# Output projection in 512-column form with its second half tile by tile between the norms, the MLP begun on three token tiles, and three reorderings at earlier boundaries

## The chip, the core and the metric

One core of a Trainium2 chip runs the whole program. The metric is the device time of one execution in microseconds (us).

## The reference, cut to what matters

One layer over 512 prompt tokens and 8 x 16 sample tokens, 640 in all, that is five tiles of 128, with 1024 channels:

```python
xn = rms_norm(x, norm_mix_pre);  z = xn @ w_in            # split into the inputs of three branches
y_fox = forgetting attention (8 heads);  y_lru = gated linear recurrence;  y_gla = gated linear attention
mix = sum_r sigmoid(gate_r(xn)) * (y_r @ w_branch[r])
mix = mix @ w_out                                          # the output projection
x = x + rms_norm(mix, norm_mix_post)
hn = rms_norm(x, norm_mlp_pre)
x = x + rms_norm(square(relu(hn @ w_up)) @ w_down, norm_mlp_post)
```

Keys, values, log forgets, convolution tails and recurrent states are outputs as well.

## The kernel before

Each engine runs its own list in order and waits on semaphores. Every fp32 product is made of three matmuls of a high and a low part (activations `XH`, `XL` or `YH`, `YL`; weights `WH`, `WL`). A weight block of 0.5 MB goes through one of two slots `s`: SP loads it into `raw[s]`, ACT casts it to `WH[s]` (`hi`, L1060), DVE subtracts for `WL[s]` (`lo`, L1465). SP loads block b+2 when `lo` of b is done; `hi` of b+2 waits until PE has finished block b. Blocks are numbered in program order.

`block` (L564) is the common form: a 128-column block of weights stays in the array and 320 tokens move, 24 matmuls for each half `h` of the tokens into `Z[0]` and `Z[1]` (PSUM banks 0 and 1). `down` (L955) is the other form: 128 tokens stay, 512 columns of weights move, one block holds two channel tiles (`kp`) of 512 columns, and the five tiles of tokens have a bank each, `DBK` (banks 2 to 6).

**Start.** Five tiles are normed and turned into `XH`, `XL` (`norm_turn` L580, `norm_hi` L1072, `norm_lo` L1471). Block 0 gives the forget inputs. PE then turns the cached log forgets (`cp_raw`, L595), and DVE copies them (L1518) and sums them up (L1521, a scan). Blocks 1 to 3 are q, k and v of head 0. After block 1 PE turns the log forgets `lfT`, after block 2 their sums `cT`. SP's list: loads 1 and 2, a wait for the sums (`ff_c`) and their store to `nc_new`, `nc_past`, load 3, head 0's cached keys (four DMAs, L364), the two stores of the log forgets (L417, L418), load 4, a wait for these stores, head 0's cached values and the sums back as rows (L359, L371 to L374), load 5. In block 4 head 0's attention begins: DVE does `lo` of block 5, key transposes (L1548), then the soft maximum; PE's `turn_p` (L669) waits for it (L1591).

**Merges.** After each branch `merge_begin(r)` runs two blocks of gates, and `merge(r)` alternates blocks `y_r @ w_branch` with gate blocks; its first branch block waits for the whole `y_r`. Before `merge(1)` PE turns `last` (L775), the recurrence's final columns, and ACT copies them to `LS` (L1275) for four stores.

**Output projection.** `MIX` is split into `YH`, `YL` (L1387, L1859). Eight blocks of `block` give the product transposed, ACT copies each into `OTB`, and PE turns every token tile back (`natural`, L918) into two banks. For each tile then: `root` on ACT (square with sum L1081, root L1082), scaling on DVE (L1874), the add to `X2` on POOL (L1024; the last tile's on DVE, L1885), a second `root`, scaling for the MLP (`normed`, L1483), `norm_turn`, `norm_hi`, `norm_lo`.

**MLP.** Four groups of eight `up` blocks (L940, 320 tokens moving) and eight `down` blocks. `up` waits for three tiles before its first half and for all five before its second.

Of the kernel before, what the change touches and what calls it, by code (L numbers as in the profile page):

```python
# [25 lines left out]
P = 128  # L26
# [70 lines left out]
def build(nc, ins, outs):  # L97
# [50 lines left out]
    with ExitStack() as ctx:  # L148
# [70 lines left out]
        def sems(names):  # L219
# [39 lines left out]
        mix_hi, mix_split, nat_pe, nat_free, x_again, nat_root, x2_ready, x2_last, x2_root = sems(  # L259
            "mix_hi mix_split nat_pe nat_free x_again nat_root x2_ready x2_last x2_root")  # L260
# [20 lines left out]
        (WG, LG, GQ, TG, Y2, RA, RX, AA, TH, A2, MM, UU, HH, XC, XP, LS) = carve(  # L281
            A0, (2, P), (T,), (T,), (T,), (T,), (T,), (T,), (T,), (T,), (T,), (T,), (T,), (T,), (T,), (XPW + 1,), (D,))
# [9 lines left out]
        OTB, X2, G1, G2, G3 = carve(A0, (KT, T), (NT, D), (D,), (D,), (D,))  # L292
        HS1, NJ, TM = carve(0, (2, D), (D,), (2, D))
# [5 lines left out]
        DBK = bank[2:7]  # L299

# [26 lines left out]
        ORD = (0, 1, 4, 2, 3)  # L327


        @blk.sync  # L330
        def _(sp):
# [77 lines left out]
            sp.wait_ge(ff_c, 1)  # L409
            sp.dma_start(nc_new, ncT[0:FOX_HEADS, :]).then_inc(scr_out, 16)  # L410
            sp.wait_ge(cp_scan, 1)
            sp.dma_start(nc_past, cpast[0:FOX_HEADS, :].rearrange("h (b s) -> h b s", s=PAST)).then_inc(scr_out, 16)
            load(Lin(B_FOX + 2), (B_FOX + 2) % 2, w_fox(Lin(0), 2))
            for q in range(P // TB):
                load_cache_k(slice(0, 1), 0, q)
            sp.wait_ge(lfn_sb, 1)
            sp.dma_start(flf_p[0, 0].rearrange("(t p) h -> p t h", p=P), lfn[:, 0:NTP, :]).then_inc(stored, 16)  # L417
            sp.dma_start(flf_s[0].rearrange("b t h -> (b t) h"), lfn[:, NTP, :]).then_inc(stored, 16)  # L418
            load(Lin(B_FOX + 3), (B_FOX + 3) % 2, w_fox(Lin(1), 0))
# [133 lines left out]
        def _(pe):  # L553
# [1423 lines left out]
```

## Time and profile before

| what | value |
|---|---|
| median of three runs | 1577.84 us (1577.53 to 1578.05) |
| the profiled execution, its own time | 1578.37 us |
| span of its trace | 1576.6 us |
| PE busy | 1508.9 us, 96% |
| DVE, ACT, POOL busy | 692.0, 622.2, 34.3 us |
| DMA | 143.41 MB, 91 GB/s over the span |

The span runs from the first to the last instruction in the trace; the own time has 1.8 us more around it. PE is busy in nearly all of the span, so what can be moved is where it is not, and where its clock is at the lower of two levels (a granted clock of 0.50 is 1.2 GHz, 1.00 is 2.4 GHz).

### The profile page before, as it was taken

Reading aid. Unit: us, or ns where it says so; the run is one execution under the profiler, and the core shown is the slowest. Engines: PE = TensorE matmul, PEld = TensorE weight load, DVE = VectorE, ACT = ScalarE, POOL = GpSimd, SP = SyncE. Lnnn points to the kernel's source line nnn. Section 1 sums busy time; section 2 is a strip of 40 time slices with the busy share of each in tenths; the row PEclk is TensorE's granted clock in tenths of the full one; section 3 lists DMA queues with packets and bytes.
Section 4 is the critical chain, followed back from the end, with each engine's and each line's share of the span. In section 5 each row is a group of like instructions: output and inputs, shape, how many; then the busy total and the mean of one; then the engine's idle time right before and its main releaser. Section 6 shows DMA issues by size and latency. Waiting matters only on the chain.

```text
span 1576.6 us, 26085 instructions
## 1 busy us (share of the span) xinstructions
PE 1508.9 (96%) x9854; PEld 1411.0 (89%) x9854; DVE 692.0 (44%) x1189; ACT 622.2 (39%) x1123; POOL 34.3 (2%) x39
## 2 busy tenths in 40 slices
PE   6799999999999989999999999997799999999996
PEld 6799999889999979998998899997798998998985
DVE  7355555532368762334445442333532322323234
ACT  6133333321277751244464432134451341431523
POOL 1000000000000000000000000001100000000003
PEclk9899999999999989999999999998799999999998
DMA  3976778222222212232332232521122222222222
GB/s 115 163 147 147 154 154 154 76 78 80 71 60 68 82 54 80 71 104 73 96 110 88 75 92 73 186 68 40 39 68 80 80 79 68 80 80 69 78 80 80
DMA packets 281350, 143.41 MB, mean 91 GB/s; under 512 B 73654, under 2 KB 268919, under 8 KB 281292
## 3 DMA queue, kind: packets, MB, share of 16 engines
q1 hardware_dynamic: 281300, 142.72, 34.5%
q8 instruction: 34, 0.56, 0.2%
q14 instruction: 16, 0.13, 0.0%
HBM read 129.86 MB, written 12.84 MB: 91 GB/s over the span
## 4 chain that ended last, share of the span: by engine, by line
PE 82%; DVE 8%; ACT 4%; issue 3%; DMA 1%; SPq 1%; DVEq 0%; ACTq 0%; POOL 0%
PE psum L564 45%; PE psum L940 14%; PE psum L955 14%; PE psum L658 1%; PE psum L688 1%; DMA w_raw<-in_w_in_dram 1%; DVE arena L1483 1%; DVE arena L1725 1%; ACT arena L1232 1%; DVE arena L1780 1%; PE psum L669 1%; PE psum L877 1%; PE psum L875 1%; PE psum L630 1%; ACT w_hi L1060 1%
## 5 line engine op out<-in xcount | busy, mean ns | idle before, releaser
L564 PE MATMUL psum<-XH,w_hi 128*128 128x320 f32 x1424 | 453.8, 319 | 6.5 <-DVE w_lo L1465 3.6
L564 PE MATMUL psum<-XH,w_lo 128*128 128x320 f32 x1424 | 443.6, 311 | 0.0
L564 PE MATMUL psum<-XL,w_hi 128*128 128x320 f32 x1424 | 443.4, 311 | 0.0
L1465 DVE TENSOR_TENSOR w_lo<-w_raw,w_hi 128x1024 fp32r<-128x1024 f32 x185 | 226.4, 1224 | 417.8 <-ACT w_hi L1060 417.0
L1060 ACT CAST w_hi<-w_raw 128x1024 fp32r<-128x1024 f32 x185 | 193.6, 1047 | 338.2 <-PE psum L955 166.3
L564 PEld LDWEIGHTS psum<-XH,w_hi 128*128 128x128 f32 x1424 | 270.9, 190 | 18.9 <-issue 9.8
L564 PEld LDWEIGHTS psum<-XL,w_hi 128*128 128x128 f32 x1424 | 270.9, 190 | 0.6
L564 PEld LDWEIGHTS psum<-XH,w_lo 128*128 128x128 f32 x1424 | 270.5, 190 | 0.0
L564 PE MATMUL psum<-YH,w_hi 128*128 128x320 f32 x512 | 160.4, 313 | 3.1 <-DVE YL L1859 2.0
L940 PE MATMUL psum<-XH,w_hi 128*128 128x320 f32 x512 | 159.1, 311 | 1.5 <-DVE fix L1929 1.5
L564 PE MATMUL psum<-YL,w_hi 128*128 128x320 f32 x512 | 159.6, 312 | 0.0
L564 PE MATMUL psum<-YH,w_lo 128*128 128x320 f32 x512 | 159.6, 312 | 0.0
L940 PE MATMUL psum<-XL,w_hi 128*128 128x320 f32 x512 | 158.9, 310 | 0.0
L940 PE MATMUL psum<-XH,w_lo 128*128 128x320 f32 x512 | 158.8, 310 | 0.0
L955 PE MATMUL psum<-w_lo,YH 128*128 128x512 f32 x320 | 124.5, 389 | 0.0
L955 PE MATMUL psum<-w_hi,YH 128*128 128x512 f32 x320 | 124.5, 389 | 0.0
L955 PE MATMUL psum<-w_hi,YL 128*128 128x512 f32 x320 | 124.5, 389 | 0.0
L1065 ACT ACTIVATE arena<-psum 128x320 f32<-128x320 f32 (+1 forms) x112 | 48.5, 434 | 145.1 <-PE psum L564 145.0
L564 PEld LDWEIGHTS psum<-YH,w_hi 128*128 128x128 f32 x512 | 97.6, 191 | 4.0 <-issue 3.5
L940 PEld LDWEIGHTS psum<-XH,w_hi 128*128 128x128 f32 x512 | 96.8, 189 | 2.0 <-DVE fix L1929 1.9
L564 PEld LDWEIGHTS psum<-YL,w_hi 128*128 128x128 f32 x512 | 97.5, 190 | 0.0
L1906 DVE TENSOR_TENSOR YL<-arena,YH 128x320 f32 x64 | 31.5, 492 | 150.3 <-ACT YH L1422 150.3
(254 smaller groups left out, 1748.7 us busy)
## 6 DMA issues: line engine op xcount, KB each, us to landing
w_raw<-in_w_in_dram SPq DMA_DIRECT2D x88, 512.0 KB, 3.7
w_raw<-in_w_up_dram SPq DMA_DIRECT2D x32, 512.0 KB, 4.0
w_raw<-in_w_down_dram SPq DMA_DIRECT2D x32, 512.0 KB, 3.5
w_raw<-in_w_branch_dram SPq DMA_DIRECT2D x24, 512.0 KB, 3.8
arena<-in_cache_fox_k_dram SPq DMA_DIRECT2D x32, 256.0 KB
arena<-in_cache_fox_v_dram SPq DMA_DIRECT2D x8, 1024.0 KB
out_dram<-arena SPq DMA_DIRECT2D x26, 256.0 KB, 2.5
arena<-in_state_gla_dram SPq DMA_DIRECT2D x4, 1024.0 KB, 5.4
```

The lines of the kernel that those rows point to most:

```text
L564: mm = pe.matmul(Z[h][:, 0:HT], w[s][:, k, :], x[:, k, h * HT:(h + 1) * HT], start=(k == 0 and i == 0), stop=(k == KT - 1 and i == 2))
L630: mm = pe.transpose(TBK[j % 2][:, (i - 4 * j) * P:(i - 4 * j + 1) * P], src[:, par, tok(i % NT)], idf[:, :])
L658: pe.matmul(S[:, 0:w], QT[:, par, tok(t)], KTt[:, par, 0:w], start=True, stop=False)
L669: mm = pe.transpose(TBK[2][:, i * P:(i + 1) * P], SP[:, p % 2, i * P:(i + 1) * P], idf[:, :])
L688: mm = pe.matmul(O[:, 0:P], KVN[:, i, :], pt[:, i * P:(i + 1) * P], start=(i == 0), stop=(i == t))
L875: pe.matmul(O[:, 0:GLA_DV], AT[:, t, :], VN[:, t, :], start=True, stop=False)
L940: mm = pe.matmul(Z[h][:, 0:HT], w[s][:, k, :], x[:, k, h * HT:(h + 1) * HT], start=(k == 0 and i == 0), stop=(k == KT - 1 and i == 2))
L955: mm = pe.matmul(DBK[t], y[:, 2 * kp + k, tok(t)], w[s][:, k, :], start=(kp == 0 and k == 0 and i == 0), stop=(kp == KP - 1 and k == 1 and ...
L1060: act.copy(WH[s][:, :, :], raw[s][:, :, :]).then_inc(w_hi, 1)
L1065: act.activation(dst, Z[h][:, 0:HT], ACT.Copy, scale=scale).then_inc(z_free[h], 1)
L1465: dve.tensor_tensor(WL[s][:, :, :], raw[s][:, :, :], WH[s][:, :, :].bitcast(F32), ALU.subtract).then_inc(w_lo, 1)
L1906: dve.tensor_tensor(YL[:, bass.ds(i * 2 + s, 1), half], UQ[:, half].unsqueeze(1), YH[:, bass.ds(i * 2 + s, 1), half].bitcast(F32), ALU.sub ...
```

## The change

The output projection takes the form of `down`. `out_first` makes the first 512 output columns of all five tiles in `DBK`; `out_second(t)` makes the other 512 for one tile at a time in `Z[(t + 1) % 2]`. The second half's four weight blocks all stay resident: two in the slots, two in the columns of `XH`, `XL` that belong to tiles 3 and 4 (`spare`), which are not needed until those tiles are normed. The tiles come out in natural order, so `OTB` and `natural` go. Squares of the first halves are summed ahead (`out_sq`, `out_bias`); each tile's norms run on ACT and DVE while PE makes the next tiles, with `norm_turn(t - 2)` inside `out_second(t)`. POOL's adds go to DVE. The first two `up` blocks start on their first token half between the norms of tiles 3 and 4.

The three reorderings: at the start the cached log forgets are turned before block 0, `lfT` and `cT` are turned inside block 2, and SP issues load 3, head 0's keys and load 4 ahead of the stores of the sums; `merge` begins with `late_block`, which makes all but the last channel tiles of both halves before it waits for the rest of `y_r`; the turning and storing of `last` moves behind `merge(1)`, its buffer `LS` into the gates' tile, and the next branch no longer waits for those stores.

```diff
 # PE, start
+            for j in CP_ORD:                       # (2, 3, 0, 1)
+                pe.wait_ge(nt_free, 2 * NT if j < 2 else 2 * NT - 2)
+                ... four transposes of cp_raw into bank[2 + j], cp_pe
             block(Lin(0), 0, XH, XL)
-            ... sixteen transposes of cp_raw
             block(Lin(1), 1, XH, XL)
-            ... transposes of lfT
-            block(Lin(2), 0, XH, XL)
-            ... transposes of cT
+            block(Lin(2), 0, XH, XL, (turn_lf, None))   # turn_lf: waits ff_lf, turns lfT; waits ff_c, turns cT
             block(Lin(3), 1, XH, XL)
 # SP, start
-            sp.wait_ge(ff_c, 1); sp.dma_start(nc_new, ...); sp.wait_ge(cp_scan, 1); sp.dma_start(nc_past, ...)
             load(Lin(B_FOX + 2), ...)
             for q in range(P // TB): load_cache_k(slice(0, 1), 0, q)
+            load(Lin(B_FOX + 3), ...)
+            sp.wait_ge(cp_scan, 1); sp.dma_start(nc_past, ...); sp.wait_ge(ff_c, 1); sp.dma_start(nc_new, ...)
             sp.wait_ge(lfn_sb, 1)
             sp.dma_start(flf_p ...); sp.dma_start(flf_s ...)
-            load(Lin(B_FOX + 3), ...)
 # DVE, start: cp8 is negated before the scan of c8; lo(Lin(3)) comes before the copy of lfn
 # PE, merges
+            def late_block(b, s, y_sem, early, y_early, y_count):
+                pe.wait_ge(w_lo, (b + 1).v)
+                for ks in (range(early), range(early, KT)):
+                    pe.wait_ge(y_sem, y_count if ks.stop == KT else y_early)
+                    for h in range(2):
+                        if ks.start == 0: pe.wait_ge(z_free[h], b.v)
+                        for k in ks: ... three matmuls into Z[h]
+                        if ks.stop == KT: mm.then_inc(z_done[h], 1)
-            merge(0, y_done, 5 * FOX_HEADS)
+            merge(0, y_done, FOX_HEADS - 1, 5 * (FOX_HEADS - 1), 5 * FOX_HEADS)
+            merge(1, yl_done, LRU_N - 1, LRU_N - 1, LRU_N)      # now ahead of the transposes of last
-            merge(1, yl_done, LRU_N)
-            merge(2, gy_done, 2 * GLA_H)
+            merge(2, gy_done, 2 * (GLA_H - 1), 2 * (GLA_H - 1), 2 * GLA_H)
 # ACT, merge(1): its two tanh of gate block 1 move ahead of the wait for h_ready; the copy to LS follows merge(1)
 # PE, output projection
+            def out_first(kp):
+                b = B_OUT + kp
+                pe.wait_ge(w_lo, b + 1); pe.wait_ge(mix_split, 2 * kp + 2)
+                for t in range(NT):
+                    for k in range(2): ... three matmuls, 512 columns, into DBK[t]
+                    if kp == KP - 1 and t < NT - 1: mm.then_inc(out_a, 1)
+                mm.then_inc(z_done[1], 1)
+            def out_second(t):
+                if t >= 2: pe.wait_ge(out_free, t - 1)
+                order = (2, 3, 0, 1) if t == NT - 1 else (0, 1, 2, 3)
+                for at_, kp in enumerate(order):
+                    if t >= 2 and at_ == (2 if t == NT - 1 else 3): norm_turn(1, t - 2, HS1)
+                    for k in range(2):           # kp < 2: the weights are the slices spare(XH), spare(XL), 2 x 256 columns
+                        ... three matmuls, 512 columns, into OUTB[t]
+                    if t == NT - 1 and kp >= 2: mm.then_inc(z_done[1], 3 if kp == 2 else 1)
+                mm.then_inc(out_b, 1)
+            pe.wait_ge(out_free, NT - 1); pe.wait_ge(nt_free, 2 * NT + 2 * 3); pe.wait_ge(w_lo, B_MLP + 1)
+            up_half(B_MLP, B_MLP % 2, 0, UBK[0][0])
+            norm_turn(1, 3, HS1)
+            pe.wait_ge(w_lo, B_MLP + 2)
+            up_half(B_MLP + 1, (B_MLP + 1) % 2, 0, UBK[1][0])
+            norm_turn(1, 4, HS1)
+            pe.wait_ge(nt_free, 4 * NT)
+            for s in range(2): up_half(B_MLP + s, (B_MLP + s) % 2, 1, UBK[s][1])
 # ACT, output projection
+            for d in range(1, KP): hi(Lin(B_OUT + d), ...)
+            for kp in range(KP): ... hi of the second half's blocks; kp < 2 into spare(XH), the others after out_first(kp)
+            root_table()
+            for t in range(NT): ... square of DBK[t] with sum into SS
+            for t in range(NT + 1):
+                if t < NT: ... out_b: square of OUTB[t] with sum, root with bias HBIAS -> out_root
+                if t in (NT - 2, NT - 1): hi(Lin(B_MLP + t - (NT - 2)), ...)
+                if t >= 1: norm_hi(1, t - 1)
+                if t < NT: act.wait_ge(x2_ready, t + 1); root(X2[:, t, :], NJ[:, :], t, x2_root)
 # DVE, output projection
+            for t in range(NT + 1):
+                if t >= 1: dve.wait_ge(x2_root, t); normed(1, t - 1, X2[:, t - 1, :], G2[:, :], HS1)
+                if t < NT:
+                    dve.wait_ge(out_root, t + 1); rinv(t)
+                    ... two scalings of 512 columns into TM -> out_free; add of TM to X2 -> x2_ready
+                if t in (NT - 2, NT - 1): lo(Lin(B_MLP + t - (NT - 2)), ...)
+                if t >= 1: norm_lo(1, t - 1)
```

## Rows read from the trace of the kernel before

**Rows 1.** The page: PE's busy tenths in 40 slices of 39.4 us; groups of instructions (busy, mean ns).

```profile
PE   6799999999999989999999999997799999999996
...
L1465 DVE TENSOR_TENSOR w_lo<-w_raw,w_hi 128x1024 fp32r<-128x1024 f32 x185 | 226.4, 1224 | 417.8 <-ACT w_hi L1060 417.0
```

**Rows 2.** Busy time by stretch; the last three columns are granted clock, DMA share, GB/s.

```profile
55.10:58.40 3.30, 3.30 (x15) 3.30 (x14) 0.00 (x0) 0.00 (x0) 0.00 (x0) 0.50 1.47 121
316.00:323.30 7.30, 4.38 (x56) 3.61 (x56) 4.55 (x11) 2.48 (x7) 0.00 (x0) 1.00 0.38 110
...
1086.00:1119.80 33.80, 15.40 (x80) 13.05 (x80) 25.89 (x39) 22.24 (x44) 10.65 (x5) 0.65 0.00 0
1119.90:1123.20 3.30, 3.30 (x12) 3.30 (x13) 1.23 (x1) 0.09 (x1) 2.97 (x1) 0.50 0.10 29
1128.00:1175.00 47.00, 47.00 (x323) 47.00 (x322) 14.97 (x20) 25.17 (x47) 0.00 (x0) 1.00 0.22 67
1180.00:1230.00 50.00, 50.00 (x222) 41.44 (x221) 14.73 (x17) 8.14 (x8) 0.00 (x0) 1.00 0.23 75
```

**Rows 3.** PE in order of time: start, us, what; in brackets the idle time before it.

```profile
54.18 0.42 PE L564 MATMUL psum<-XH,w_hi 128*128 128x320 f32 x1 [1.42 <-DVE w_lo L1465]
...
78.54 0.33 PE L669 MATMUL psum<-ident,arena 128*128 128x128 f32 x1 [3.67 <-DVE arena L1591]
...
323.33 0.41 PE L564 MATMUL psum<-YH,w_hi 128*128 128x320 f32 x1 [1.06 <-DVE YL L1596]
...
578.27 1.87 PE L775 MATMUL psum<-ident,last 128*36 128x128 f32 x8 [6.39 <-DVE fix L1745]
```

**Rows 4.** SP's DMA issues in order of time, 45 to 65 us.

```profile
47.75 7.13 SPq L364 DMA_DIRECT2D arena<-in_cache_fox_k_dram  x4
54.92 3.16 SPq L417 DMA_DIRECT2D out_dram<-arena  x1
...
60.39 0.38 SPq L359 DMA_DIRECT2D arena<-in_cache_fox_v_dram  x1
...
64.84 3.08 SPq L336 DMA_DIRECT2D w_raw<-in_w_in_dram  x1
```

**Rows 5.** ACT in order of time, 30 to 92 us.

```profile
38.37 0.74 ACT L1115 ACTIVATE arena<-arena 8x640 f32<-8x640 f32 x1
...
72.66 1.05 ACT L1060 CAST w_hi<-w_raw 128x1024 fp32r<-128x1024 f32 x1 [8.39 <-DMA w_raw<-in_w_in_dram]
```

**Rows 6.** DVE in order of time, 30 to 92 us.

```profile
36.66 4.41 DVE L1521 TENSOR_TENSOR_SCAN arena<-arena 8x2048 f32<-8x2048 f32 x1
...
46.86 0.18 DVE L1534 COPY arena<-psum 128x40 f32<-128x40 f32 x1
```

**Rows 7.** ACT at the boundary between the recurrence and merge(1).

```profile
571.89 0.74 ACT L1255 ACTIVATE arena<-arena 128x640 f32<-128x640 f32 x1
...
577.19 1.28 ACT L1128 ACT_TABLE_LOAD   x1
578.48 0.77 ACT L1128 ACTIVATE gates<-psum 128x320 f32<-128x320 f32 x2
```

**Rows 8.** Groups of instructions, 1086 to 1120 us: busy, mean ns, idle before.

```profile
L1483 DVE SCALAR_TENSOR_TENSOR arena<-arena,small 128x1024 f32<-128x1024 f32 x5 | 11.0, 2204 | 0.2
L580 PE MATMUL psum<-ident,arena 128*128 128x128 f32 x40 | 9.0, 397 | 13.8 <-DVE XL L1471 9.1 <-DVE arena L1483 4.7
...
L1471 DVE TENSOR_TENSOR XL<-psum,XH 128x512 fp32r<-128x512 f32 x10 | 6.6, 682 | 1.4 <-ACT XH L1072 1.4
L1874 DVE SCALAR_TENSOR_TENSOR arena<-psum,small,arena 128x1024 f32<-128x1024 f32 x5 | 6.4, 1283 | 0.2
...
L1072 ACT CAST XH<-psum 128x512 fp32r<-128x512 f32 x10 | 5.8, 586 | 4.8 <-PE psum L580 4.8
L1081 ACT ACTIVATE arena<-arena 128x1024 f32<-128x1024 f32 x5 | 5.2, 1048 | 4.1 <-POOL arena L1024 2.7 <-DVE arena L1885 1.3
...
L1885 DVE TENSOR_TENSOR arena<-arena 128x1024 f32<-128x1024 f32 x1 | 1.2, 1225 | 0.0
```

More of the change, by code:

```diff
@@ L299, in build, with spare, by_256, norm_bank @@
         DBK = bank[2:7]
+        OUTB = [Z[(t + 1) % 2] for t in range(NT)]
+        UBK = ((Z[0], Z[1]), (DBK[0], DBK[1]))
+        def spare(v, kp, k, n=2):
+            return v[:, 4 * kp + 2 * k:4 * kp + 2 * k + n, T - 256:T]
+        def by_256(v):
+            return v[:, :, :].rearrange("p k n -> p (k n)").rearrange("p (a b) -> p a b", b=256)
+        def norm_bank(n, t, q):
+            if n == 0:
+                return bank[2 + 2 * (t % 2) + q]
+            return DBK[t] if q == 0 else bank[7]
         blk = ctx.enter_context(nc.Block())
@@ new lines, in _, with up_half @@
+            for kp in range(KP):
+                out_first(kp)
+            for t in range(NT):
+                out_second(t)
+            def up_half(b, s, h, bk):
+                for k in range(KT):
+                    for i, (w, x) in enumerate(((WH, XH), (WH, XL), (WL, XH))):
+                        mm = pe.matmul(bk[:, 0:HT], w[s][:, k, :], x[:, k, h * HT:(h + 1) * HT],
+                                       start=(k == 0 and i == 0), stop=(k == KT - 1 and i == 2))
+                mm.then_inc(z_done[h], 1)
@@ L1255, in lru_window @@
                     act.activation(MM[:, :], MM[:, :], ACT.Sqrt).then_inc(m_act, 1)
+                if not cur:
+                    for h in range(2):
+                        gate(1, Lin(1), b + 1, 1, h)
                 if cur:
@@ L1271, in _ @@
             lru_window(Lin(LRU_N), False, True)
[L1272 to L1273 removed]
+            merge(1)
             act.wait_ge(last_pe, 1)
+            act.wait_ge(mix_sum, 2 * KT)
             act.copy(LS[0:36, :], psum[0:36, 2:4, :].rearrange("p a b -> p (a b)")).then_inc(last_sb, 1)
[L1276 removed]
             def o_copy(h):
@@ new lines, in group @@
+            def group(g, last=False, done=0):
+                b = g * (2 * KT) + B_MLP
+                with step.loop(KT // 2 - done, 4) as i:
+                    for s in range(2):
+                        bb = (b + 2 * done).loop(2, i) + s
+                        hi(bb + 1, (b.c + s + 1) % 2)
+                        for h in range(2):
+                            up_half(Z[h], bb, bass.ds(i * 2 + (s + 2 * done), 1), (g * KT + 2 * done).loop(2, i) + s, h)
+                with step.loop(KT // 2 - last, 0) as i:
+                    for s in range(2):
+                        hi((b + KT).loop(2, i) + (s + 1), (b.c + KT + s + 1) % 2)
```

357 lines of the change are left out of this document (196 added, 161 removed).

## Prediction, made before the changed kernel was run

> **What bounds the kernel now.** I read the page first: PE is busy in nine tenths or more of nearly every slice, and the slices that fall short are the first three and two near 1100 us, with dips at the branch boundaries [rows 1]. So the kernel is bound by PE, and only PE's empty stretches, and those at the lower clock, can be won. The stretches by windows give their size. From 1086.0 to 1119.8 us PE is busy for 15.4 of 33.8 us, and with turning tiles only: this is the norms between output projection and MLP, where DVE has 25.9 and ACT 22.2 us of work [rows 2]. Then PE in order of time, read for the brackets: idle 3.67 us before 78.54, 1.06 before 323.33, 6.39 before 578.27 [rows 3]. Last SP's issues, because what PE waits for at 78.54 hangs on a load.
>
> Two prices serve throughout. In full stretches at a granted clock of 1.00, leaving out the one record cut off at each end, a 320-column matmul takes 47/321 = 0.146 us and a 512-column one 50/220 = 0.227 us [rows 2]. And idling can cost clock: behind an idle time of 1.42 us [rows 3] the clock stood at 0.50 for 3.3 us, and again behind the norms; in a stretch whose three gaps make 2.92 us, 1.06 of them the last, it stayed at 1.00 [rows 2, 3]. A stretch at the lower clock costs half its length, 1.6 us. Between none and one for each gap of 1 to 2 us, I count two for three.
>
> **Start.** Before, load 5 lands at 72.64 (its cast starts at 72.66), and 5.9 us later, at 78.54, PE gets head 0's first softmax tile: cast, `lo`, two key transposes, two soft maxima, one scaling, all queued on ACT and DVE behind that load [rows 3, 5]. What sets load 5 is SP: four key DMAs (7.13 us of issue), a store that takes 3.16 us to issue, load 4, a wait for the stores until the values go out at 60.39, load 5 at 64.84 [rows 4]. After the change the keys and loads 3 and 4 are issued from 24 to 38 us, beside PE's first blocks. SP is next needed when the copy of the log forgets (46.86 + 0.18 = 47.04) is done [rows 6]. That copy moves little. Before, DVE's scan ended at 41.07, `lo` 1.23 behind it, so the chain from there to the copy was 47.04 - 42.3 = 4.7 us [rows 1, 6]. After, the scan is done early and the chain starts with ACT's logarithm, which ended at 39.11 [rows 5]; block 0 starts some 1.4 us later (most of the sixteen transposes now stand before it, the same number less behind it), and `lo` 3 now stands in the chain: 39.1 + 1.4 + 4.7 + 1.2 = 46.4. From there SP needs 60.39 - 54.92 = 5.5 us to the values, so 51.9 [rows 4]. Load 5's landing is bounded: if the transfers take as long as from 60.39 to 72.64, 64.2; if only SP's issue (4.45 us later, 56.4) and the quickest load of some 4 us count, 60.5. I take the middle, 62.3: DMA was full there, and load 4's 0.5 MB, which overlapped the beginning of that stretch, is gone from it. PE gets its tile at 68.2, 10.3 us earlier; load 6 can come up to 0.8 us late for block 6, and I take off 0.7. **9.6 us won**, 7.6 to 12.1 by the bounds. The idle times before blocks 2 to 4 go too but are no extra: PE waits at the softmax tile instead, from about 64.
>
> **Merges 0 and 2.** `late_block` fills the 1.06 us before 323.33 with 42 matmuls that don't need the last head [rows 3]. At merge 2 PE does not wait, so nothing is won. Splitting off the last channel tile puts both halves' ends only 3 x 0.146 us apart, so the next block's first half waits for DVE's gating of the bank (about 0.5 us against 0.44): 0.1 to 0.2 us twice. **0.6 us won**, 0.3 to 1.1.
>
> **Merge 1.** PE was free at 578.27 - 6.39 = 571.9 [rows 3]. `late_block` needs both banks free, that is ACT's tanh of gate block 1, which now follows the square root (ends 572.63), with a table load of 1.28 and 0.4 us: 574.4 [rows 7]. Its 42 early matmuls last 6.2 us, beyond 578.1, when the last channel is split. So PE idles 2.5 us rather than 6.4 and then turning, and a stretch at 0.50 follows in both cases. The first branch block begins at 574.4 rather than 579.8 (after eight transposes): 5.4 us, and the eight transposes return after the merge for about 1.0 at full clock [rows 8]. The copy to `LS`, 1 us on ACT, delays the cast of the second block behind it, which has most of a 7 us block as cover; without that cover it would cost 1 us. The four stores on SP stand behind loads that run two blocks ahead. **4.4 us won**, 2.5 to 6.0.
>
> **Output projection and norms.** Before: 384 matmuls x 0.1464 = 56.2, the empty stretch 33.8, the stretch at 0.50 behind it 1.6: 91.6 us [rows 2].
>
> After: `out_first` is 120 x 0.227 = 27.2 us, begun about 0.7 us later because it waits for two split tiles, not one. Call its end S. ACT then has one cast 1.05, the root's table 1.5, five squares of 0.85: S + 6.9. So tile 0's second square starts at S + 7.1, though its matmuls end at S + 5.5. Per tile: ACT square with root 1.0; DVE scaling 1.28 in two parts and 0.2 for the reciprocal, add 1.23; ACT second root 1.5; DVE `normed` 1.28 and 0.2; PE eight transposes 1.0 (9.0/5 us at a clock of 0.65); ACT casts 0.59 each; DVE `XL` 0.68 each [rows 8]. (The mean of 2.2 us for `normed` has POOL's adds beside it. These go to DVE, so I take 1.28, its shape's time at L1874, and keep 2.2 as the bound.)
>
> The ring that repeats is add, second root, `normed`, scaling, add: 1.5 + 1.5 + 1.5 + 1.23 + hand-overs = 5.9 us. PE's share of a tile is 24 x 0.227 + 1.0 = 6.45. So from tile 2 on PE sets the pace: `out_second(4)` ends at S + 10.9 + 3 x 6.45 = S + 30.2. Then three gaps. Tile 3's add ends at S + 29.1, `lo` of the first `up` block and tile 2's two `XL` follow it on DVE: PE starts at S + 31.7, gap 1.5. `up` half 3.5, transposes 1.0: 36.2. Tile 4's add ends at 35.9, `lo` of the second block behind it: 37.2, gap 1.0. `up` half, transposes of tile 4: 41.7; its casts and `XL`: 43.4, gap 1.7. There the second halves begin and 48 matmuls of the MLP (7.0 us) are done. The rest of the MLP sees the same queues; the second-half weights' casts and loads have 6.8 us a block against a load of 4 and 2.3 for the two casts.
>
> Sum after: 0.7 + 27.2 + 43.4 - 7.0 + two stretches at 0.50 3.2 = 67.5. **24.1 us won.** Bounds: no stretch at 0.50 27.3; `normed` at 2.2 (the same recurrence gives S + 46.7) and three of them 19.2. The second half's weights in `spare` move as two runs of 256; no row shows that form. Nearest below is 0.227, above it two 320-column matmuls, 0.293, which on 60 matmuls would cost 4 us; a run of 256 is still contiguous, so I take nothing.
>
> Here a rule speaks for a larger gain. The rows show 0.227 us for each 512-column matmul with its own weight load [rows 2]. The Trainium skill, page "TensorE: Matmul & The Clock Gate", section "Back-to-back issue gap", gives about 131 ns as the sustained spacing at 512 columns in a real kernel. By that, 240 matmuls take 31.4 us rather than 54.5, and the sum would end 23 us lower (an estimate from that page). The 512-column matmuls of `down` in this trace don't bear it out, so it gets no chance of its own.
>
> **Sum.** 9.6 + 0.6 + 4.4 + 24.1 = 38.7 us. Against the profiled execution's own 1578.37 (span 1576.6 and 1.8 around it) that is 1539.7; the median of the runs lies 0.53 lower, so **1539 us**. All lows together give 29.6 (1548), all highs 46.5 (1531).
>
> **Rivals.** (a) The norms set the pace. DVE carries more than before, and the ring has only 0.5 us to spare against PE. If its memory-to-memory work stays at 2.2 us a tile, and the add is as slow as that too, each tile loses about 2 us more than PE hides: 8 us, 1547. For it: L1483's mean; against: POOL, beside which it was slow, falls idle. Chance 0.15. (b) The start is bound by DMA. Between 55 and 58 us the DMA share is over 1.4 [rows 2]; if load 5 lands 12.3 us after a later 55, not 62.3, only about 5 us are won there: 1544. Against it: the keys are gone from that stretch. Chance 0.12. (c) The short gaps cost no clock, in the tail and at merge 1: 3.2 + 1.6 less, 1534. For it, the stretch at 316. Chance 0.12. (d) Slower: the clock stays at 1.2 GHz through the projection. Each 512-column matmul would take some 0.2 us longer; about 190 of the 240 eat up the 39 us, and all of them give 1588 without the tail's fill. Against it: `down` holds 1.00 in the same form [rows 2]. Chance 0.02. (e) A wait I have not seen ties the projection to the old order, and only the other parts remain small: no change, 0.02.
>
> **How the numbers follow.** The forecast has 0.57, with a range of its own from 1534 to 1544. With (a), (b) and (c) the range 1529 to 1548 leaves out under 2 in 10. A measurement of this kernel can tell about 0.2%, 3 us: faster 0.96, same 0.02, slower 0.02.
>
> **What would show it.** Right: the span's two weak slices near 1100 disappear, three PE gaps of 1 to 2 us stand before the first full `up`, load 5's cast starts near 62, PE's idle time before merge 1 is near 2.5 us. Wrong: idle times inside `out_second` on `normed` (a), load 5's cast beyond 65 (b), clock below 1.00 in `out_first` (d). The weakest numbers are the landing of load 5 and how many gaps cost clock.

## The result and the profile after

| | before | after |
|---|---|---|
| median of four runs | 1577.68 us | 1534.03 us (1532.94 to 1537.67) |
| ratio, 95% interval | 1 | 0.9727 (0.971 to 0.9744) |
| profiled execution: own time, span | 1578.37, 1576.6 us | 1532.94, 1531.2 us |
| mean granted clock in it | 0.980 | 0.994 |

The change made the kernel faster, by 43.7 us in the medians and 45.4 us between the two spans. The profiled execution of after is the quickest of its four, and that of before (1578.37) lies above its four timed runs (1577.4 to 1578.05), so what is read from the two traces comes out 1.7 us larger than the medians. The executions of after whose clock is listed at 0.994, 0.994 and 0.991 had spans of 1531.2, 1532.2 and 1536.0 us; by an estimate, clock alone would make 0.003 x 1531 = 4.6 of the 4.8 us between the first and the last.

First the page of after, PE's slices and the grant, to set against [rows 1]; then PE of after in order of time, with the idle time in brackets, to set against [rows 3].

```profile
PE   6899999999999999999999999999999999999996
...
PEclk9999999999999999999999999999999999999999
```

```profile
67.74 0.47 PE L691 MATMUL psum<-ident,arena 128*128 128x128 f32 x1 [4.18 <-DVE arena L1687]
...
306.66 0.55 PE L691 MATMUL psum<-ident,arena 128*128 128x128 f32 x3 [1.60 <-DVE arena L1687]
...
554.06 0.39 PE L583 MATMUL psum<-XH,w_hi 128*128 128x320 f32 x1 [0.54 <-ACT gates L1200]
563.97 0.38 PE L769 MATMUL psum<-YH,w_hi 128*128 128x320 f32 x1 [2.63 <-ACT gates L1200]
...
900.03 1.28 PE L826 MATMUL psum<-ident,arena 128*128 128x128 f32 x10 [0.17 <-DVE arena L1876]
...
1013.18 0.47 PE L954 MATMUL psum<-w_hi,YH 128*128 128x512 f32 x1 [2.74 <-DVE YL L1955]
...
1071.65 0.38 PE L997 MATMUL psum<-XH,w_hi 128*128 128x320 f32 x1 [1.02 <-DVE XL L1566]
...
1076.91 0.42 PE L997 MATMUL psum<-XH,w_hi 128*128 128x320 f32 x1 [0.63 <-DVE w_lo L1560]
...
1083.13 0.42 PE L997 MATMUL psum<-XH,w_hi 128*128 128x320 f32 x1 [1.56 <-DVE XL L1566]
```

The two weak slices near 1100 us are gone; in their place stand three gaps that make 3.21 us. The same rows of before, and one pair ahead of merge 2, give the milestones. The row at 316.41 in before and 306.66 in after is the last head's softmax tile; it is called the later window below.

```profile
316.41 0.55 PE L669 MATMUL psum<-ident,arena 128*128 128x128 f32 x3 [1.60 <-DVE arena L1591]
...
564.61 0.38 PE L564 MATMUL psum<-XH,w_hi 128*128 128x320 f32 x1 [0.54 <-ACT gates L1128]
...
914.94 1.28 PE L786 MATMUL psum<-ident,arena 128*128 128x128 f32 x10 [0.17 <-DVE arena L1780]
...
1027.34 0.39 PE L564 MATMUL psum<-YH,w_hi 128*128 128x320 f32 x1 [2.00 <-DVE YL L1859]
...
1119.86 0.64 PE L940 MATMUL psum<-XH,w_hi 128*128 128x320 f32 x1 [1.47 <-DVE fix L1929]
```

| term | forecast | measured | from the rows |
|---|---|---|---|
| start | 9.6 | 9.75 | 316.41 - 306.66 |
| merges 0 and 2 | 0.6 | 0.80 | (564.61 - 554.06) less the start, all of it at merge 0: 914.94 - 900.03 = 14.91 ahead of merge 2, 14.90 behind it |
| merge 1 | 4.4 | 4.35 | (1027.34 - 2.00) - (1013.18 - 2.74) = 14.90, less the two above |
| output projection and norms | 24.1 | 30.5 | 45.4 less 14.90 |

The rest of the MLP is the same in both: from the last rows shown to the end it takes 1576.6 - 1119.86 = 456.7 us before, of which 1.6 are a stretch at the lower clock, and 1531.2 - 1083.13 = 448.1 after, which has 7.0 us of the MLP behind it by then. So the 30.5 belong to the stage.

Last, the queues and stretches of after that answer [rows 4, 5, 6, 8] and [rows 2]: SP's issues, ACT's cast of load 5, DVE's copy of the log forgets; groups of DVE in the tail; windows, whose last three columns are granted clock, DMA share and GB/s.

```profile
24.57 7.29 SPq L382 DMA_DIRECT2D arena<-in_cache_fox_k_dram  x4
...
45.65 0.39 SPq L436 DMA_DIRECT2D out_dram<-arena  x1
...
49.12 0.38 SPq L377 DMA_DIRECT2D arena<-in_cache_fox_v_dram  x1
...
52.67 4.21 SPq L354 DMA_DIRECT2D w_raw<-in_w_in_dram  x1
...
61.86 1.05 ACT L1132 CAST w_hi<-w_raw 128x1024 fp32r<-128x1024 f32 x1 [5.73 <-DMA w_raw<-in_w_in_dram]
...
45.44 0.18 DVE L1631 COPY arena<-psum 128x40 f32<-128x40 f32 x1
```

```profile
L1566 DVE TENSOR_TENSOR XL<-psum,XH 128x512 fp32r<-128x512 f32 x10 | 6.4, 685 | 2.0 <-ACT XH L1144 1.9
L1578 DVE SCALAR_TENSOR_TENSOR arena<-arena,small 128x1024 f32<-128x1024 f32 x5 | 6.4, 1285 | 0.2
L1988 DVE TENSOR_TENSOR arena<-arena 128x1024 f32<-128x1024 f32 x5 | 6.1, 1226 | 0.2
```

```profile
68.00:72.00 4.00, 4.00 (x17) 4.00 (x17) 1.50 (x5) 1.80 (x3) 0.00 (x0) 0.50 1.19 177
...
564.00:568.00 4.00, 4.00 (x18) 4.00 (x19) 3.21 (x7) 1.82 (x3) 0.30 (x1) 0.62 0.00 0
...
1013.20:1040.40 27.20, 27.20 (x120) 22.51 (x121) 11.43 (x12) 8.56 (x10) 0.00 (x0) 1.00 0.32 110
1040.40:1070.40 30.00, 30.00 (x146) 24.89 (x144) 20.50 (x39) 19.14 (x43) 0.00 (x0) 1.00 0.08 24
...
1072.00:1080.00 8.00, 7.37 (x53) 7.12 (x52) 7.43 (x10) 3.04 (x6) 0.00 (x0) 1.00 0.40 112
1080.00:1088.00 8.00, 6.44 (x46) 6.19 (x45) 2.27 (x4) 4.71 (x10) 4.37 (x1) 1.00 0.05 15
```

PE is busy through both halves of the projection without an idle row, and `normed` takes 1.285 us now that POOL does not add beside it, against 2.204 in [rows 8]. The grant is 1.00 through the tail in spite of its three gaps, and 0.50 to 0.62 behind the gaps at the softmax and at merge 1.

### The profile page after: what moved, and what is told of

Its sections match the earlier page's. It is cut to its first block, busy times and chain, and to the rows that moved or that the text cites. A ratio compares the mean times of both kernels' runs of the same rounds, so it can differ in the third digit from the quotient of the medians.

```text
span 1531.2 us, 25519 instructions
## 1 busy us (share of the span) xinstructions
PE 1487.6 (97%) x9670; PEld 1381.6 (90%) x9670; DVE 693.1 (45%) x1199; ACT 616.0 (40%) x1117; POOL 24.9 (2%) x35
## 4 chain that ended last, share of the span: by engine, by line
PE 84%; DVE 6%; ACT 4%; issue 3%; DMA 1%; SPq 0%; DVEq 0%; ACTq 0%
PE psum L583 41%; PE psum L997 15%; PE psum L1031 14%; PE psum L954 2%; PE psum L769 1%; PE psum L980 1%; PE psum L680 1%; PE psum L710 1%; DMA w_raw<-in_w_in_dram 1%; ACT arena L1304 1%; PE psum L691 1%; DVE arena L1876 1%; DVE arena L1821 1%; PE psum L917 1%; PE psum L915 1%
## 5 line engine op out<-in xcount | busy, mean ns | idle before, releaser
L1132 ACT CAST w_hi<-w_raw 128x1024 fp32r<-128x1024 f32 x181 | 189.6, 1048 | 317.7 <-PE psum L1031 166.4
L583 PEld LDWEIGHTS psum<-XL,w_hi 128*128 128x128 f32 x1424 | 268.5, 189 | 0.6
L583 PEld LDWEIGHTS psum<-XH,w_lo 128*128 128x128 f32 x1424 | 268.1, 188 | 0.0
L583 PE MATMUL psum<-YH,w_hi 128*128 128x320 f32 x336 | 103.8, 309 | 0.0
L583 PE MATMUL psum<-YL,w_hi 128*128 128x320 f32 x336 | 103.8, 309 | 0.0
L583 PE MATMUL psum<-YH,w_lo 128*128 128x320 f32 x336 | 103.8, 309 | 0.0
L997 PEld LDWEIGHTS psum<-XL,w_hi 128*128 128x128 f32 x512 | 96.1, 188 | 0.1
L997 PEld LDWEIGHTS psum<-XH,w_lo 128*128 128x128 f32 x512 | 96.1, 188 | 0.0
L1998 DVE TENSOR_TENSOR YL<-arena,YH 128x320 f32 (+1 forms) x64 | 31.5, 492 | 140.9 <-ACT YH L1504 140.8
L1137 ACT ACTIVATE arena<-psum 128x320 f32<-128x320 f32 x96 | 41.6, 434 | 114.8 <-PE psum L583 114.7
```

The lines of the kernel that those rows point to most:

```text
L583: mm = pe.matmul(Z[h][:, 0:HT], w[s][:, k, :], x[:, k, h * HT:(h + 1) * HT], start=(k == 0 and i == 0), stop=(k == KT - 1 and i == 2))
L997: mm = pe.matmul(bk[:, 0:HT], w[s][:, k, :], x[:, k, h * HT:(h + 1) * HT], start=(k == 0 and i == 0), stop=(k == KT - 1 and i == 2))
L1132: act.copy(WH[s][:, :, :], raw[s][:, :, :]).then_inc(w_hi, 1)
L1137: act.activation(dst, Z[h][:, 0:HT], ACT.Copy, scale=scale).then_inc(z_free[h], 1)
L1998: dve.tensor_tensor(YL[:, j, half], UQ[:, half].unsqueeze(1), YH[:, j, half].bitcast(F32), ALU.subtract).then_inc(u_done[h], 1)
```

## Experiments

Each kernel is the changed kernel with one edit. "Against after" is the ratio less 0.9727, times 1577.7 us; an interval of a ratio is about 2 us wide to each side, and after's own 2.7, so small differences are read from the milestones of the traces, one execution each.

| kernel | median, us | ratio to before, 95% interval | against after, us |
|---|---|---|---|
| start_undone | 1543.88 | 0.9785 (0.977 to 0.98) | +9.2 |
| start_queue_undone | 1542.13 | 0.9768 (0.9755 to 0.9782) | +6.5 |
| start_engines_undone | 1536.13 | 0.9733 (0.972 to 0.9746) | +0.9 |
| full_wait | 1537.85 | 0.9746 (0.9733 to 0.9759) | +3.0 |
| no_cover | 1569.54 | 0.9948 (0.9933 to 0.9963) | +34.9 |
| up_after_five | 1542.11 | 0.9769 (0.9756 to 0.9782) | +6.6 |
| adds_on_pool | 1538.87 | 0.9748 (0.9735 to 0.9762) | +3.3 |
| lo_on_pool | 1534.54 | 0.9727 (0.9714 to 0.9741) | 0.0 |
| softmax_first | 1530.45 | 0.9701 (0.9687 to 0.9714) | -4.1 |
| gate_early | 1530.69 | 0.97 (0.9687 to 0.9713) | -4.3 |
| combined | 1527.08 | 0.968 (0.9667 to 0.9693) | -7.4 |
| combined_two | 1527.09 | 0.9679 (0.9666 to 0.9692) | -7.6 |

**The start, undone whole (start_undone).** SP, PE and DVE issue the start in the order of before: the two edits below, together.

> Only the start is put back (SP's order, the transposes of the cache's prefix behind the block of load 3, the DVE order with -c and the low part of block 3); the rest is the changed kernel. Theory, that the three reorderings are worth what the milestones show (first window of the later heads at 306.7 instead of 316.4): about +9.7 us on the changed kernel, ratio to the kernel before near 0.9789, load 5's cast back near 72.7, softmax idle back from 4.18 near 3.7. Rival, that the parts of the change depend on each other (the later stages give back some of the start): +5 or less. Rival, that the start's gain is lost downstream and the projection made it all: under +1.

Load 5's cast came at 72.27, the softmax tile at 78.15 behind 3.71 us of idle time, and the later window, at 306.66 in after, came at 316.04: 9.4 us later. The time agrees. The start is worth what its milestones show, and nothing of it is lost later.

**Which part of the start (start_queue_undone, start_engines_undone).** The first puts back SP's order alone:

```diff
+            sp.wait_ge(ff_c, 1)
+            sp.dma_start(nc_new, ncT[0:FOX_HEADS, :]).then_inc(scr_out, 16)
+            sp.wait_ge(cp_scan, 1)
...
             load(Lin(B_FOX + 2), (B_FOX + 2) % 2, w_fox(Lin(0), 2))
             for q in range(P // TB):
                 load_cache_k(slice(0, 1), 0, q)
-            load(Lin(B_FOX + 3), (B_FOX + 3) % 2, w_fox(Lin(1), 0))
-            sp.wait_ge(cp_scan, 1)
...
+            load(Lin(B_FOX + 3), (B_FOX + 3) % 2, w_fox(Lin(1), 0))
```

> Of the three reorderings at the start only SP's is put back (the stores of -c ahead of the loads of block 4 and of the keys, the load of block 5 last); TensorE's and DVE's stay new. Theory, that the order of the queue carries the 9.8 us of the start and the two others only make the stores ready early: most of it comes back, +5 to +9 on the changed kernel, load 4 issued near 45 instead of 37.5. Rival, that the early -c is what counts: the stores then wait hardly longer than before and it is 0 to +3.

The second puts back PE's order (the transposes between whole blocks again) and DVE's, and leaves SP's new. On DVE:

```diff
-            step(dve.tensor_scalar(cp8, cp8, -1.0, None, ALU.mult))
-            dve.tensor_tensor_scan(c8, rn8, c8, 0.0, ALU.mult, ALU.add).then_inc(cp_scan, 1)
-            dve.wait_ge(cp_scan, 1)
+            step(dve.tensor_tensor_scan(c8, rn8, c8, 0.0, ALU.mult, ALU.add))
             dve.tensor_scalar(nc8, c8, -1.0, None, ALU.mult).then_inc(ff_c, 1)
-            lo(Lin(3), 1)
+            dve.tensor_scalar(cp8, cp8, -1.0, None, ALU.mult).then_inc(cp_scan, 1)
...
+            lo(Lin(3), 1)
```

> The other two reorderings at the start are put back (TensorE's transposes of the cache's prefix behind blocks of loads, DVE's -c and its low part of block 3 in the old order); SP's new order stays. Theory, that queue and engines are both needed: -c comes some 4 us later, and with it the stores, the values and load 5 that stand behind them on SP, so +3 to +6. If the queue alone carries the start: 0 to +2. If the engines carry it: +8 to +10.

```profile
45.94 0.40 SPq L354 DMA_DIRECT2D w_raw<-in_w_in_dram  x1
46.38 7.12 SPq L382 DMA_DIRECT2D arena<-in_cache_fox_k_dram  x4
53.54 2.87 SPq L435 DMA_DIRECT2D out_dram<-arena  x1
```

These are SP's issues with its order put back (start_queue_undone): the keys and a load stand behind -c again, at 46 us instead of 24, and the store after them takes 2.87 us. SP stood 24.5 us in its wait for -c. The softmax tile came at 77.21, the later window at 315.81, 9.15 us behind after; the time's +6.5, with 2 to 3 us to each side, does not contradict that.

With only the engines put back, that window came at 308.75, 2.1 us behind, and load 5's cast at 64.98. My +3 to +6 for it was too much, and its reason was wrong: -c was ready at 45.30 instead of 44.38, 0.9 us later and not 4. SP's first store went out at 46.47 instead of 43.89, because the negation of the past's sums now follows -c. What held SP longest behind the stores was another wait: 4.2 us for the turned sums, since PE turns them behind block 2 again, so the values went out at 52.58 instead of 49.12. Of the 3.1 us by which the cast is late, 1.0 is made up before the later window. So the queue's order carries the start: alone it wins 316.04 - 308.75 = 7.3 of the 9.4 us. The engines' order is worth 2.1 us with the queue new, and 9.4 - 9.15 = 0.25 with the queue old.

**Merges without the early beginning (full_wait).**

```diff
-                late_block(Lin(B_MG[r] + 2), s, y_sem, early, y_early, y_count)
+                pe.wait_ge(y_sem, y_count)
+                block(Lin(B_MG[r] + 2), s, YH, YL)
```

> The last branch block of each of the three merges waits for the whole Y again, instead of beginning on the contraction tiles that are done. Theory, that merge 1 won by beginning early: its first row comes at about 567.6 instead of 563.97, so +3.6 there, +0.8 at merge 0, 0 at merge 2, together +4 to +5 (ratio near 0.9755); the one gap before merge 1 is longer, near 6.2 instead of 2.63. Rival, that merge 1 won because another piece of work was moved behind, not because of the early beginning: under +1.5 in all.

```profile
568.80 0.64 PE L583 MATMUL psum<-YH,w_hi 128*128 128x320 f32 x1 [6.28 <-DVE YL L1834]
```

PE waits 6.28 us at merge 1 instead of 2.63. From the later window to the projection's first matmul this kernel takes 1018.41 - 307.12 = 711.29 us, after 1013.18 - 306.66 = 706.52: 4.8 us, of which 0.7 lie ahead of merge 1 (there a gap of 0.68 us is back at merge 0). The time's +3.0, with 2 to 3 us to each side, does not contradict that. So 4.8 of the 5.15 us that the merges won hang on the early beginning; moving other work behind won little without it.

**The second halves without their cover (no_cover).** Same instructions; a tile's transposes stand ahead of the next tile's second half.

```diff
+                if 1 <= t < NT - 1:
+                    norm_turn(1, t - 1, HS1)
                 order = (2, 3, 0, 1) if t == NT - 1 else (0, 1, 2, 3)
...
-                    if t >= 2 and at_ == (2 if t == NT - 1 else 3):
-                        norm_turn(1, t - 2, HS1)
+                    if t == NT - 1 and at_ == 2:
+                        norm_turn(1, t - 1, HS1)
...
-            norm_turn(1, 3, HS1)
```

> The transposes of tile t-1 stand in front of the second half of tile t for tiles 1 to 3, and in the middle of it for tile 4, so that the matmuls of one tile no longer run under the norm of the tile ahead; forms and counts of all instructions are the same. Theory, that the projection stage won by this cover: the chain from a tile's last matmul to its norm is 7.0 us on ACT and DVE (from the square at 1047.53 to the norm's end at 1054.48), three times 7 in full and about 3.8 for tile 4, so +22 to +27, and 3 to 6 more if the gaps drop the clock, 1556 to 1567 in all. Rival, that the 512-column form won most of it: +10 or less.

PE in order of time, and two windows:

```profile
1054.26 1.94 PE L599 MATMUL psum<-ident,arena 128*128 128x128 f32 x8 [8.52 <-DVE arena L1579]
...
1086.53 1.94 PE L599 MATMUL psum<-ident,arena 128*128 128x128 f32 x8 [7.08 <-DVE arena L1579]
...
1102.32 1.97 PE L599 MATMUL psum<-ident,arena 128*128 128x128 f32 x8 [5.02 <-DVE arena L1579]
```

```profile
1056.00:1064.00 8.00, 7.00 (x25) 5.31 (x24) 0.00 (x0) 0.93 (x4) 0.00 (x0) 0.82 0.00 0
1064.00:1072.00 8.00, 1.91 (x9) 1.94 (x10) 5.45 (x8) 2.46 (x6) 0.00 (x0) 0.61 0.01 2
```

From the first projection matmul to the full first `up` halves it takes 106.8 us (1012.82 to 1119.61) instead of 69.95: 36.8 us more. Six gaps (8.52, 7.08, 7.08, 5.02 and, before the full halves, 1.63 and 1.56) make 30.9 us instead of 3.2, so 27.7 are idle time and 9.1 the rest, with a grant of 0.54 to 0.90 in the seven windows of 8 us from 1048 to 1104. The cover is worth more than the 30.5 us that the stage won in all: with the 512-column form and tiles one by one, but without the cover, the stage would be some 6 us longer than before. (In this order every tile waits for the whole norm of the one ahead; a kernel planned without cover would not have to.) The form alone gives little: at the prices of [rows 2], 240 matmuls of 512 columns take 54.5 us and the 384 of 320 columns 56.2. My estimate was 22 to 27 us for the idle time, and for the clock a third to two thirds of what it took.

**The first `up` halves after all five tiles (up_after_five).**

```diff
+            norm_turn(1, 3, HS1)
+            norm_turn(1, 4, HS1)
+            pe.wait_ge(nt_free, 4 * NT)
...
             up_half(B_MLP, B_MLP % 2, 0, UBK[0][0])
-            norm_turn(1, 3, HS1)
...
             up_half(B_MLP + 1, (B_MLP + 1) % 2, 0, UBK[1][0])
-            norm_turn(1, 4, HS1)
-            pe.wait_ge(nt_free, 4 * NT)
```

> The first halves of the two first MLP blocks (two times 3.5 us of matmuls) come only after the transposes of all five tiles, instead of between them. Theory, that they cover the norms of tiles 3 and 4 fully: +6.5 to +7.5 us, and up to 1.6 more if the long gap drops the clock; the gaps of 1.02, 0.63 and 1.56 become gaps that sum to 10 or so. Rival, that the tail is set elsewhere (the loads of the MLP or DVE's low parts): 0 to +3.

The gaps became 2.59, 5.24 and 1.40 us, 9.2 in all instead of 3.2, and from 1080 to 1088 the grant was 0.50. The 7.0 us of the MLP are real cover for tiles 3 and 4.

**Is the ring of the norms close to PE (adds_on_pool)?** The five additions go back to POOL, 2.4 us each instead of 1.23.

```diff
+            for t in range(NT):
+                pool.wait_ge(out_free, t + 1)
+                pool.tensor_tensor(X2[:, t, :], X2[:, t, :], TM[:, :], ALU.add).then_inc(x2_ready, 1)
...
-                    dve.tensor_tensor(X2[:, t, :], X2[:, t, :], TM[:, :], ALU.add).then_inc(x2_ready, 1)
```

> The five additions to x of the tiles are made on POOL as in the kernel before (there 2.35 us for one, on DVE 1.23), the rest is the changed kernel. Theory, that TensorE's 6.45 us for a tile set the pace and the norms' ring runs beside it with little to spare: the ring grows by 1.1 to 2.2 us per tile, past 6.45, so +3 to +8 us, with idle rows inside the second halves. Rival, that the ring has more slack than I think: 0 to +2, only the last tile's addition showing.

```profile
1058.00 2.40 POOL L1100 TENSOR_TENSOR arena<-arena 128x1024 f32<-128x1024 f32 x1 [4.63 <-DVE arena L1988]
1065.03 2.40 POOL L1100 TENSOR_TENSOR arena<-arena 128x1024 f32<-128x1024 f32 x1 [4.63 <-DVE arena L1988]
1072.06 3.31 POOL L1100 TENSOR_TENSOR arena<-arena 128x1024 f32<-128x1024 f32 x1 [4.63 <-DVE arena L1988]
```

POOL's additions stand 7.0 us apart: that is the ring, now longer than PE's 6.45. In after the same additions of DVE are 5.8 us apart between the first two (ends at 1051.45 and 1057.27). PE's gaps in the tail make 7.2 us instead of 3.2. So the norms were 0.6 us per tile away from setting the pace (rival (a)), as the forecast's 5.9 against 6.45 said.

**The low parts of the first two MLP blocks on POOL (lo_on_pool).**

```diff
-                    lo(Lin(B_MLP + t - (NT - 2)), (B_MLP + t - (NT - 2)) % 2)
...
+                pool.wait_ge(w_hi, B_MLP + d + 1)
+                pool.tensor_tensor(WL[s_][:, :, :], raw[s_][:, :, :], WH[s_][:, :, :].bitcast(F32), ALU.subtract).then_inc(w_lo, 1)
```

> The low parts of the first two MLP blocks (two subtractions of 1.23 us on DVE) are made on POOL. Theory, that DVE sets the gaps of 1.02, 0.63 and 1.56 us in the tail: they shrink by 1 to 2 us together, -1 to -2. Rival, that POOL is slower at it (2.3 us and more), and slows DVE's reads of the norm beside it (2.20 instead of 1.28 us where POOL added beside it in the kernel before): 0 to +2.

```profile
1062.74 1.23 DVE L1994 TENSOR_TENSOR arena<-arena 128x1024 f32<-128x1024 f32 x1
...
1068.85 2.41 DVE L1994 TENSOR_TENSOR arena<-arena 128x1024 f32<-128x1024 f32 x1
```

The subtraction ran on POOL from 1067.78 for 2.40 us, and DVE's addition that started at 1068.85 took 2.41 us instead of 1.23: it ended 1.1 us behind POOL's end, about as if it had begun only then. What DVE was relieved of it lost in waiting. The gaps are 1.10, 0.34 and 1.56 us, and nothing is won.

**Two orders at the remaining gaps (softmax_first, gate_early, combined, combined_two).** In softmax_first ACT's cast and DVE's low part of load 5 stand behind head 0's first soft maxima; in gate_early the first half of gate block 1's tanh stands ahead of the square root. ACT's part of both:

```diff
+                first = not a.terms and a.c == 0
+                if not first:
                     hi(b + 1, 1 - s)
                 take(0, 0)
                 exps(0)
                 exps(1)
                 take(0, 1)
+                if first:
+                    hi(b + 1, 1 - s)
...
                     act.activation(A2[:, :], AA[:, :], ACT.Square).then_inc(a_act, 1)
+                if not cur:
+                    gate(1, Lin(1), b + 1, 1, 0)
...
-                    for h in range(2):
-                        gate(1, Lin(1), b + 1, 1, h)
+                    gate(1, Lin(1), b + 1, 1, 1)
```

> In head 0's window ACT's cast and DVE's low part of load 5 stand behind the first two soft maxima instead of ahead of them. Theory, that the one gap of 4.18 us at the start (softmax at 67.74) is only that order: the gap shrinks to under 1 us and the clock of 0.50 in 68 to 72 goes, so -3.5 to -5 us on the changed kernel, 1529 to 1530.5. Rival, that the cast then comes too late for the block that needs load 5, and a gap of like size opens there: 0 to -1. Rival, that the inputs of the softmax themselves come late: 0.

> ACT makes the first half of gate block 1's tanh ahead of the square root that stands in front of it at the seam before merge 1, instead of behind it. Theory, that the gap of 2.63 us before merge 1 is ACT's order: the gap shrinks to about 0.4, -2.2 us, and -1.6 more if the clock of 0.62 in 564 to 568 was its price: 1530.3 to 1532. Rival, that the square root then comes as much later for the branch: 0.

```profile
66.43 0.41 PE L583 MATMUL psum<-XH,w_hi 128*128 128x320 f32 x1 [2.17 <-DVE w_lo L1564]
```

```profile
568.30 0.41 PE L769 MATMUL psum<-YH,w_hi 128*128 128x320 f32 x1 [0.39 <-DVE YL L1834]
```

These are softmax_first, then gate_early. In softmax_first the gap at the softmax is gone, and one of 2.17 us opened at the block that needs load 5: half of the theory and half of its rival. The later window came at 303.81, 2.85 us sooner. In gate_early the gap at merge 1 fell from 2.63 to 0.39 and the grant from 564 to 572 is 1.00; from the later window to the projection this kernel takes 703.64 us instead of 706.52, 2.9 us less, between the two sizes expected. Both orders are gains, and they add:

> The two orders that shortened a gap, together: load 5's cast and low part behind the first soft maxima, and the first half of gate block 1's tanh ahead of the square root. Theory, that the two gaps stand at different places and add up: -3.6 and -3.35 on the changed kernel, near 1527. Rival, that the second is partly used up by the first: 1528.5 to 1530.

> As the kernel with both orders, and ACT's cast of load 5 stands between the second exponentials and the eviction that it stood behind (it started at 64.08 while load 5 had landed at 61.86, and DVE was idle until 65.15). Theory: the gap of 2.17 us that was left at the start goes to under 0.7, with it the clock of 0.70 to 0.88 in 64 to 72, so -2 to -3.5 more, 1523.5 to 1525. Rival, that DVE's soft maxima or the head's inputs then hold the block: 0 to -1 more.

The two gains of 4.1 and 4.3 make 7.4 in combined; by the milestones 2.85 and 2.9 make 1013.18 - 1007.35 = 5.8. Both combined kernels beat before and after, and they can't be told from each other. In combined_two the cast stands one line higher:

```diff
+                if first:
+                    hi(b + 1, 1 - s)
                 take(0, 1)
-                if first:
-                    hi(b + 1, 1 - s)
```

This last edit did what it was for at its place, but the 2 to 3.5 us more that I expected did not come, and the trace shows where the gain went in the profiled execution. PE of combined and a window, then the same of combined_two:

```profile
1007.35 0.47 PE L954 MATMUL psum<-w_hi,YH 128*128 128x512 f32 x1 [2.74 <-DVE YL L1963]
...
1065.80 0.38 PE L997 MATMUL psum<-XH,w_hi 128*128 128x320 f32 x1 [1.05 <-DVE XL L1571]
```

```profile
1008.00:1012.00 4.00, 4.00 (x19) 3.27 (x18) 4.00 (x6) 2.78 (x4) 0.00 (x0) 1.00 0.00 0
```

```profile
65.06 0.42 PE L583 MATMUL psum<-XH,w_hi 128*128 128x320 f32 x1 [0.50 <-DVE w_lo L1565]
...
77.10 0.55 PE L691 MATMUL psum<-ident,arena 128*128 128x128 f32 x3 [1.46 <-DVE arena L1692]
...
1006.00 0.56 PE L954 MATMUL psum<-w_hi,YH 128*128 128x512 f32 x1 [2.74 <-DVE YL L1963]
...
1066.05 0.38 PE L997 MATMUL psum<-XH,w_hi 128*128 128x320 f32 x1 [1.02 <-DVE XL L1571]
```

```profile
1004.00:1008.00 4.00, 2.00 (x5) 1.63 (x6) 4.00 (x7) 4.00 (x8) 0.00 (x0) 0.78 0.01 2
1008.00:1012.00 4.00, 4.00 (x15) 3.21 (x14) 3.40 (x5) 1.40 (x2) 0.00 (x0) 0.79 0.00 0
```

The gap of 2.17 us fell to 0.50, another of 1.46 opened at 77.10, and the projection begins 1.35 us sooner. But behind the same idle time of 2.74 us the grant stood below 1.00 here and at 1.00 in combined, so from its first matmul to the first `up` it took 60.05 us instead of 58.45, and the lead was gone. Whether the timed runs, whose medians tie, lost it in the same way was not seen.

## Why the prediction was right, and where it was off

**What bounds the kernel.** Right: from before to after, PE's idle time fell from 67.7 to 43.6 us (span less busy time), 24.1 of the 45.4, and the other 21.3 are busy time, at a mean grant of 0.994 instead of 0.980. The number is less good than the mechanism: 1534.03 us lies 5 us under the 1539 forecast, at the very edge of the forecast's own range from 1534 to 1544.

**Start.** The term held (9.75 for 9.6), with two errors that nearly cancel. SP began to issue load 5 at 52.67 rather than 56.4: the copy of the log forgets was done 0.8 us sooner than I said, and SP needed 3.5 us from there to the values (45.62 to 49.12), not 5.5: the store that had taken 3.16 us to issue [rows 4] took 0.39, while the wait for the stores grew to 2.4. Against that the load took 9.2 us from there to its cast, where the middle I took gave 5.9. So it landed at 61.8 for 62.3. The 5.9 us from its cast to the softmax tile held: 67.74 - 61.86. Rival (b) is there in kind, for the DMA share was 1.15 to 1.29 in 52 to 64 us and the load was slow; but it was issued early enough. What slowed the load was not tried.

**Merges.** Right in mechanism (full_wait) and in the sum. Merge 2 gave nothing, and merge 0 alone the 0.80. The idle time at merge 1 is 2.63 us where I said 2.5, and the stretch at the lower clock follows.

**Output projection and norms.** Right in mechanism (no_cover), 6.3 us too small. `out_first` took 27.2 us for 120 matmuls as said, `out_second(4)` ended at 1070.63 against a forecast of 1040.4 + 30.2 = 1070.6, and the second halves of `up` began at S + 42.7 for a forecast of S + 43.4. Two other terms of the stage's sum were mis-sized. First, "two stretches at 0.50 3.2" after: none came in this execution, in the tail or behind the 2.74 us ahead of `out_first`. That is in part luck: in five other kernels with the same projection a stretch did come behind the 2.74 us (last section). Second, "91.6 us" before: I priced the matmuls at full clock, 56.2 us, but from 1027.34 to the empty stretch at 1086.0 they take 58.7; a part of that is a stretch behind the 2.00 us at the seam, where this window of before has a grant of 0.58 (0.42 x 4 = 1.7 us); what made the other 0.8 stays open.

```profile
1028.00:1032.00 4.00, 4.00 (x18) 4.00 (x18) 4.00 (x6) 3.49 (x6) 0.00 (x0) 0.58 0.01 4
```

With the stretch behind 1119.86 that makes 94.1. So the difference is 3.2 (after's stretches) + 2.5 (before) + 0.6 (the tail, 42.7 for 43.4).

**The rivals.** (c) was half right: no clock was lost in the tail, but merge 1's stretch was paid. That the median lies at (c)'s 1534 us is luck in part: (c) gives back 3.2 + 1.6, the runs show the 3.2 without the 1.6, and 2.5 us that no rival had, from before. (a) did not come, and adds_on_pool shows how close it was. The 2.204 us that spoke for it [rows 8] was a mean of two kinds: three of the five `normed` ran beside POOL's additions and took 1.65, 3.40 and 3.40 us, the other two 1.28. (d) is out: the grant is 1.00 through the projection. (e) is out by the table above.

The Trainium skill's 131 ns for a 512-column matmul (page "TensorE: Matmul & The Clock Gate", section "Back-to-back issue gap"), which got no chance, is not borne out in after either: 27.2 us for 120 matmuls is 0.227 us each.

**What stays open.** Whether the runs that were only timed differ by the same stretch as the profiled ones was not seen; their mean clocks, listed to a thousandth, fit it.

## What to carry to other kernels

When PE is the bound, price a change of form by what it lets run underneath: here the same matmuls without the cover would have lost more than the whole stage won. Look at the queue before the engines: moving two weight loads and four key loads ahead of stores that wait won 7.3 of the 9.4 us of the start by itself. And price both sides of a difference with the same care: a stall in the old kernel has its own stretch of low clock, which goes with it.

## What the hardware showed beyond what I expected

**The same idle time does not always cost clock.** Ten of the profiled executions (after and nine of the experiments, all but no_cover, up_after_five and adds_on_pool) have the same projection behind the same 2.74 us of idle time. From its first matmul to the first `up` row it takes 58.4 to 58.5 us in five (after, lo_on_pool, softmax_first, start_queue_undone, combined) and 59.8 to 60.1 in the other five (start_undone, start_engines_undone, full_wait, gate_early, combined_two). Of the other three, no_cover and adds_on_pool have a grant of 1.00 behind this gap, up_after_five 0.76 and 0.81 in the windows from 1012 to 1020. So this gap's price was 0 or 1.6 us; what decides it was not tried. The Trainium skill, page "TensorE: Matmul & The Clock Gate", section "What's actually happening", says that the activity on which the grant rests is taken in periods that run freely, not from a kernel's own start. By that the price would hang on when the gap comes; the ten executions agree with it as far as they go, but none shows it. A forecast should carry half the price for such a gap, and a difference of 1.6 us between two kernels of this family is no finding by itself.

**POOL and DVE hold each other up, first come.** POOL's addition and DVE's `normed` of before, 1098 us:

```profile
1098.34 2.35 POOL L1024 TENSOR_TENSOR arena<-arena 128x1024 f32<-128x1024 f32 x1 [2.56 <-DVE arena L1874]
1098.37 3.40 DVE L1483 SCALAR_TENSOR_TENSOR arena<-arena,small 128x1024 f32<-128x1024 f32 x1
```

DVE began 0.03 us behind POOL and took 3.40 us instead of 1.28: it ended 1.08 us behind POOL's end, about as if it had begun there. In lo_on_pool POOL had begun, and DVE's addition took 2.41 instead of 1.23 us; in adds_on_pool DVE's subtraction had begun at 1071.89 (1.22 us), and POOL's addition from 1072.06 took 3.31 instead of 2.40. The one that came first was not slowed. Nor was DVE's subtraction for `XL`, one of whose inputs is in PSUM, beside POOL's addition at 1058.00 in adds_on_pool (1.28 us for two). The Trainium skill, page "SBUF — State Buffer", section "SBUF: two separate sides", calls the port that the two share an exclusive lock: a DVE instruction with two inputs in SBUF and a POOL instruction that reads SBUF take it in order of start, for the whole instruction. The rows agree.

**A store's issue time depended on what was in flight.** The store that takes 3.16 us on SP behind the four key DMAs [rows 4], and 2.87 and 2.95 with SP's order put back, takes 0.39 in after, where the keys went out at 24.57 and not just ahead of it. Which transfer it waits for was not tried.
